# Two layers of a hybrid trunk on one core: the opening's modulation chunks in another order, one chunk between the layers in other memory, and GpSimd's loads behind the chunks

## The reference, cut to what matters

```python
for layer in range(DEPTH):                       # DEPTH = 2
    sh1, sc1, g1, sh2, sc2, g2 = modulation(c or c_ctx, w_mod[layer], b_mod[layer])
    h = rms_norm(x, norm1[layer]) * (1 + sc1) + sh1
    o = even_mixer(h) if layer % 2 == 0 else odd_mixer(h)   # projections, attention, gating
    x = x + g1 * o
    h = rms_norm(x, norm2[layer]) * (1 + sc2) + sh2
    x = x + g2 * ec_moe(h)                       # 16 experts, each picks 64 + 16 rows
y = rms_norm(x, final_norm)
def modulation(cvec, w_mod, b_mod):
    return split(silu(cvec) @ w_mod + b_mod, 6)  # w_mod is 1024 x 6144 for each layer
```

## Time and profile before

| what | us |
|---|---|
| median of 3 runs | 1421.32 |
| lowest and highest of them | 1417.71, 1426.94 |
| the profiled execution, device time | 1414.43 |
| its span, first to last instruction | 1412.3 |
| TensorE busy in it (91%) | 1282.4 |
| VectorE busy (62%) | 877.2 |
| ScalarE busy (52%) | 735.4 |

### The profile page before, as it was taken

One profiled execution on the slowest core, in us unless ns is written; L12 is line 12 of the kernel. 1 busy time (PEld: TensorE's weight loads), 2 busy tenths in 40 slices (PEclk: granted clock), 3 DMA queues, 4 the chain that ended last, 5 costly groups with the idle time before them and its releaser, 6 DMA issues.

```text
span 1412.3 us, 18208 instructions
## 1 busy us (share of the span) xinstructions
PE 1282.4 (91%) x7552; PEld 925.0 (65%) x7552; DVE 877.2 (62%) x1010; ACT 735.4 (52%) x866; POOL 212.1 (15%) x125
## 2 busy tenths in 40 slices
PE   5899988898589999999789999899986999999996
PEld 3796766796356666666459994567954566666662
DVE  3713456524668888888374352454256699999995
ACT  3522037613557777777253214554146677777763
POOL 3000000020102222211020000000202033332220
PEclk9998799999889999999899999799998999999998
DMA  9721073004599999999794222001145999999984
GB/s 359 219 81 32 30 247 129 1 31 178 202 361 380 380 377 375 381 387 397 263 277 120 80 76 87 1 1 62 59 179 210 367 399 383 383 383 384 381 338 165
DMA packets 99606, 322.86 MB, mean 229 GB/s; under 512 B 6367, under 2 KB 30142, under 8 KB 83142
## 3 DMA queue, kind: packets, MB, share of 16 engines
q1 hardware_dynamic: 87360, 283.54, 53.4%
q0 software_dynamic: 8400, 27.58, 7.6%
q10 hardware_dynamic: 3766, 10.58, 1.9%
HBM read 298.20 MB, written 23.49 MB: 228 GB/s over the span
## 4 chain that ended last, share of the span: by engine, by line
PE 67%; DMA 14%; ACT 9%; DVE 8%; issue 2%; SPq 1%; ACTq 0%; DVEq 0%; POOLq 0%
PE psum L889 64%; DMA stage<-in_w_mod 4%; ACT arena L1719 3%; DVE w_lo L1905 3%; DVE arena L2183 2%; DMA xT<-in_moe_w_up 2%; DMA arena<-in_moe_w_up 2%; DMA stage<-in_moe_w_up 2%; ACT w_hi L1788 1%; DMA h_hi<-h_dram,arena 1%; DMA stage<-in_moe_w_gate 1%; DMA arena<-in_moe_w_gate 1%; PE psum L1372 1%; ACT arena L1485 1%; DVE h_lo L1905 1%
## 5 line engine op out<-in xcount | busy, mean ns | idle before, releaser
L889 PE MATMUL psum<-w_hi,h_hi 128*80 128x512 f32 (+1 forms) x848 | 330.2, 389 | 14.4 <-DVE h_lo L1905 10.2
L1905 DVE TENSOR_TENSOR w_lo<-stage,w_hi 128x2048 fp32r<-128x2048 f32 (+1 forms) x120 | 270.9, 2270 | 93.6 <-ACT w_hi L1498 55.9
L889 PE MATMUL psum<-w_lo,h_hi 128*80 128x512 f32 (+1 forms) x848 | 326.0, 384 | 0.0
L889 PE MATMUL psum<-w_hi,h_lo 128*80 128x512 f32 (+1 forms) x848 | 325.7, 384 | 0.0
L889 PE MATMUL psum<-h_hi,w_hi 128*128 128x320 f32 x672 | 211.9, 315 | 5.1 <-DVE h_lo L1955 5.1
L1788 ACT ACTIVATE w_hi<-stage 128x2048 fp32r<-128x2048 f32 x98 | 186.7, 1915 | 45.2 <-PE psum L889 28.7
L889 PE MATMUL psum<-h_lo,w_hi 128*128 128x320 f32 x672 | 210.1, 313 | 0.0
L889 PE MATMUL psum<-h_hi,w_lo 128*128 128x320 f32 x672 | 210.0, 312 | 0.0
L1905 DVE TENSOR_TENSOR w_lo<-arena,w_hi 128x2048 fp32r<-128x2048 f32 x75 | 171.5, 2290 | 33.5 <-ACT w_hi L1788 32.6
L889 PEld LDWEIGHTS psum<-w_hi,h_hi 128*80 128x80 f32 (+1 forms) x848 | 129.8, 153 | 88.8 <-issue 15.3
L854 POOL DMA_INDIRECT acc_dram<-arena x31 | 109.7, 3538 | 429.6 <-ACT arena L1825 230.3
(11 more groups left out here) (253 smaller groups left out, 1329.1 us busy)
## 6 DMA issues: line engine op xcount, KB each, us to landing
stage<-in_w_mod SPq DMA_DIRECT2D x48, 1024.0 KB, 7.6
stage<-in_moe_w_up SPq DMA_DIRECT2D x35, 1024.0 KB, 15.8
stage<-in_moe_w_down SPq DMA_DIRECT2D x32, 1024.0 KB, 16.4
stage<-in_moe_w_gate SPq DMA_DIRECT2D x31, 1024.0 KB, 16.0
arena<-in_moe_w_gate SPq DMA_DIRECT2D x28, 1024.0 KB, 17.4
arena<-in_moe_w_up SPq DMA_DIRECT2D x24, 1024.0 KB, 16.2
arena<-in_moe_w_down SPq DMA_DIRECT2D x21, 1024.0 KB, 14.9
xT<-in_moe_w_down SPq DMA_DIRECT2D x11, 1024.0 KB, 21.1
```

What stands on the lines that cost most here:

```text
L889: return pe.matmul(o, w, x, start=first, stop=last, skip_group_check=True)
L1905: return nc.vector.tensor_tensor(dst, src, hi.bitcast(F32), ALU.subtract)
```

## The change

The lines of the listing here are cut from the diff; the helper functions `mod_before` and `mod_place` are new.

```diff
-SUM_PLACES, OUT_PLACES, X_PLACES = (4,), (5, 6), (7, 8)
-PLACES = 9
+SUM_PLACES, OUT_PLACES, X_PLACES, FRONT_PLACE = (4,), (5, 6), (7, 8), 9
+PLACES = 10
...
-MOD_AT = {"start": [0, 1, 2, 3], "qk": [4, 5], "first scores": [6, 7], (0, "sum"): [8], (0, "root"): [9, 10],
+MOD_AT = {"start": [2, 3, 0, 1], "qk": [4, 5], "first scores": [6, 7], (0, "sum"): [8], (0, "root"): [9, 10],
...
+def mod_before(c):      # the chunk whose turning frees mrow
+def mod_place(c):       # a chunk's number in TensorE's order, for mod_used
...
-    mod("start")
+    for c in MOD_AT["start"][:2]:
+        chunk(c)
     for L in range(LAYERS):
...
         if L > 0:
-            mod("acc")
+            chunk(MOD_AT["acc"][0]), chunk(MOD_AT["acc"][1])
+            chunk(MOD_AT["acc"][2], (FRONT_PLACE, SUM_PLACES[0]))
             chunk(MOD_AT["next norm"][0])
...
+            if (kind, m) == ("q", 0):
+                for c in MOD_AT["start"][2:]:
+                    chunk(c)
...
+            if n == FRONT_PLACE:
+                return arena[:, 0:PIECE]
...
-            filled(pool, ("mod rows", 2))
+            filled(pool, ("mod rows", MOD_AT["start"][-1]))
...
                     emptied(pool, (0, "moe", KD - 1))
+                    pc = piece[("mod", MOD_AT["next norm"][1], 1)]
+                    pool.wait_ge(stage_in[pc["place"]], arrived(pc["p"]))
...
# TensorE
-            for c in MOD_AT["start"]:
-                mod_rows(c)
-                if c:
-                    turn_mod(c - 1)
-                if c == 1:
-                    norm_sum_of_two((0, "norm", 0))
+            mod_rows(scale[0])
+            mod_rows(scale[1])
+            turn_mod(scale[0])
+            turn_mod(scale[1])
+            norm_sum_of_two((0, "norm", 0))
+            mod_rows(shift[0])
+            turn_mod(shift[0])
+            mod_rows(shift[1])
             turn_mod(MOD_AT["start"][-1])
...
# ScalarE
+                    if (L, which) == (0, 0) and k in (4, 6):
+                        modulation("start", slice(k // 2 - 2, k // 2 - 1))
...
+                        if L == 0 and k == 1:
+                            modulation("start", slice(3, None))
...
             squares_for_pool(0, 0, None)
-            modulation("start", slice(0, 2))
+            split(in_keys(0)[0])
             root_of(0, 0)
             modulation("start", slice(2, 3))
-            split(in_keys(0)[0])
-            modulation("start", slice(3, None))
...
# VectorE
-                if name == (1, "norm", 0):
-                    split(in_keys(1)[0])
+                if name[1:] == ("norm", 0):
+                    split(in_keys(name[0])[0])
...
+                        if L == 0 and k == 4:
+                            modulation("start", slice(3, None))
...
-            modulation("start", slice(0, 1))
+            modulation("start", slice(0, 2))
             root_of((0, "norm", 0))
-            modulation("start", slice(1, 3))
-            split(in_keys(0)[0])
-            modulation("start", slice(3, None))
+            modulation("start", slice(2, 3))
```

More of the change, by code:

```diff
@@ L102, in turned_banks @@
     return (512, 512) if STEPS[i] is None else (512, 512, 256)
-MOD_AT = {"start": [0, 1, 2, 3], "qk": [4, 5], "first scores": [6, 7], (0, "sum"): [8], (0, "root"): [9, 10],
+MOD_AT = {"start": [2, 3, 0, 1], "qk": [4, 5], "first scores": [6, 7], (0, "sum"): [8], (0, "root"): [9, 10],
           (0, "rank"): [11], (0, "top"): [12], "acc": [13, 14, 15], "next norm": [16, 17], "cq": [18, 19], (1, "sum"): [20],
           (1, "root"): [21, 22], (1, "rank"): [23], (1, "top"): []}
+def mod_before(c):
+    start = MOD_AT["start"]
+    if c in start:
+        return start[start.index(c) - 1] if start.index(c) else None
+    return c - 1 if c - 1 not in start else start[-1]
+def mod_place(c):
+    start = MOD_AT["start"]
+    return start.index(c) + 1 if c in start else c + 1
 IN = {0: [("q", 1024), ("q", 1280), ("kv", 1536), ("va", 512), ("va", 768), ("u", 0), ("u", 256)],
@@ L173, in plan_psum @@
         one(("x", k), "dve")
-    for c in MOD_AT["start"]:
-        one(("mod rows", c), "act")
-        if c == 2:
-            one(("mod turned", 1), "dve")
-        elif c:
-            one(("mod turned", c - 1), "dve")
-        if c == 1:
-            one((0, "norm", 0), "dve", 2)
+    scale, shift = MOD_AT["start"][:2], MOD_AT["start"][2:]
+    one(("mod rows", scale[0]), "act"), one(("mod rows", scale[1]), "act")
+    one(("mod turned", scale[0]), "dve"), one(("mod turned", scale[1]), "dve")
+    one((0, "norm", 0), "dve", 2)
+    one(("mod rows", shift[0]), "act"), one(("mod turned", shift[0]), "dve"), one(("mod rows", shift[1]), "act")
     one(("mod turned", MOD_AT["start"][-1]), "dve")
@@ L321, in plan_weights, with chunk @@
     after = {"va": lambda m: ("va", m, 2), "kv": lambda m: "v", "ckv": lambda m: "kr", "cq": lambda m: ("cq", 1)}
+    def chunk(c, places=(None, None)):
+        Lc, j = divmod(c, MODS)
+        for half in range(2):
+            piece(("mod", c, half), rows(a["w_mod"][Lc])[:, 4 * half:4 * half + 4, MODC * j:MODC * (j + 1)], False,
+                  ("mod_used", mod_place(c)) if half == 0 else ("mod rows", c), places[half])
     def mod(at):
         for c in MOD_AT[at]:
-            L, j = divmod(c, MODS)
-            for half in range(2):
-                piece(("mod", c, half), rows(a["w_mod"][L])[:, 4 * half:4 * half + 4, MODC * j:MODC * (j + 1)], False,
-                      ("mod_used", c + 1) if half == 0 else ("mod rows", c))
-    mod("start")
-    for L in range(LAYERS):
-        def chunk(c):
-            Lc, j = divmod(c, MODS)
-            for half in range(2):
-                piece(("mod", c, half), rows(a["w_mod"][Lc])[:, 4 * half:4 * half + 4, MODC * j:MODC * (j + 1)], False,
-                      ("mod_used", c + 1) if half == 0 else ("mod rows", c))
+            chunk(c)
+    for c in MOD_AT["start"][:2]:
+        chunk(c)
+    for L in range(LAYERS):
         if L > 0:
-            mod("acc")
+            chunk(MOD_AT["acc"][0]), chunk(MOD_AT["acc"][1])
+            chunk(MOD_AT["acc"][2], (FRONT_PLACE, SUM_PLACES[0]))
             chunk(MOD_AT["next norm"][0])
@@ L1546, in modulation @@
                 for c in MOD_AT[at][part]:
-                    if c > 0:
-                        filled(act, ("mod turned", c - 1))
+                    if mod_before(c) is not None:
+                        filled(act, ("mod turned", mod_before(c)))
                     evacuate(("mod rows", c), mrow[:, :], bank(("mod rows", c)))
```

## The result

The changed kernel takes 1405.18 us (median; 1402.0 to 1409.7) where the kernel before takes 1420.44 in runs beside it (1417.71 to 1426.94): a ratio of 0.9882, 95% interval 0.9853 to 0.9912. (The quotient of the two medians is 0.9893, inside that interval.) That is faster by 1.2% by the ratio and by 1.1% by the medians. One run of the changed kernel took 2506.01 us and one of a repeat of the kernel before 4331.27; ranges, ratios and intervals leave them out, the two medians (1405.18, and 1422.12 of that repeat) include them and would be 1404.70 and 1420.78 without. The forecast was 1412.8, about half that gain, and I had given 0.87 to a change within 1% and 0.10 to a gain of more.

The account below looks back on a forecast made before the run. TensorE, busy 91% of the span, was taken as the bound, with its idle or low-clock time deciding; 2.3 us (opening) plus 6.2 (between the layers) made 8.5, so 1421.3 becomes 1412.8. Range 1404 to 1421, the forecast's own 1409 to 1417.

Parts of the forecast that it names:

- Opening, step 1: Opening: norm sum starts at 26.5, 0.4 us earlier, and VectorE's first step comes at 31.1 instead of 31.51.
- rival B: Clock stays up in both waits: opening 4.2 us, between the layers 8.5, sum 12.7, giving 1408.6; chance 0.11.
- Step 2: Opening: VectorE's scaling starts at 37.2, 3.4 us earlier. Between layers: sum's load 1.6 earlier, addition 0.6 faster, 2.2 together.
- Step 3: Opening: chunk 1 is late next; projection starts 41.6, 2.3 us earlier. Between layers: norm sum ends 2.6 earlier, at 712.9.
- Step 4: Opening: TensorE is slower than the tiles afterwards, so the first projection's start decides; 2.3 us taken.
- Step 5: Opening: GpSimd's loads some 3 us later cost nothing. Between layers: VectorE's first tile ends 721.6, projection starts 6.2 earlier.
- Steps 4 and 7: Between layers: chunks issued 2.2 us earlier, wait for chunk 17 goes; GpSimd's loads start at 717, costing nothing.
- Step 6: Between layers: projection ends 737.8 instead of 743.95; next weight's split, 2.6 us earlier at 737.9, just fits.
- rival C: A later load or low spell of the clock takes up the gain before the end: about 1421; chance 0.08.
- A: Between layers: clock takes the norm sum's gain, projection starts 3.6 us earlier instead of 6.2; 1415.4; chance 0.17.
- D: Clock stays at 1.2 GHz through all 96 matmuls of both first projections: 11.2 us slower, 1432.5; chance 0.06.
- E: Chunk 15's second piece lands late or ScalarE's copies hold up GpSimd: 6 to 7 us left, 1414.5; 0.58 with the forecast.

Follow-up runs that it names:

- `opening_only`: Changed kernel with the two edits between the layers taken out, only the opening's new order left: 1413.70 us, ratio 0.9938.
- `no_front`: Changed kernel with chunk 15 back in the staging slots, GpSimd's loads still behind chunk 17: 1408.38 us, ratio 0.9900.
- the two filled ones: Changed kernel with idle transposes in four waits, 1409.63 us, and with them in the two opening waits only, 1407.22 us.
- `after_again`: Changed kernel once more, unchanged, for a second trace: 1406.13 us, ratio 0.9888.
- `no_gate`: Changed kernel with GpSimd's loads between the layers no longer held back behind chunk 17: 1410.76 us, ratio 0.9924.
- `before_filled`: Kernel before with 18 idle transposes in TensorE's wait ahead of the opening's first turning of a chunk: 1422.08 us, ratio 1.0002.
- `between_only`: Kernel before with only the part between the layers (chunk 15's new place, GpSimd's loads behind chunk 17): 1410.79 us, ratio 0.9931.
- `after_third`: Changed kernel once more, unchanged, for a third trace: 1405.4 us, ratio 0.988.
- `after_filled`: Changed kernel with idle transposes in four waits of TensorE, in the opening and between the layers: 1409.63 us, ratio 0.9916.

## Why the prediction was right in its mechanisms and short in its size

**Opening, step 1** is the step that failed. It took the norm sum's 4.47 us over from the earlier trace rows. The norm sum took 2.40, in two of three traces of the changed kernel and in all four of `opening_only`, `no_front` and the two filled ones; 3.91 in `after_again` and 4.07 in `no_gate`. In the five unfilled traces of the old order it is 4.08 to 4.47. TensorE's idle time ahead of it is shorter in the new order (1.06 us in the first trace of the changed kernel, 3.13 ahead of the turning of the chunk before), and in `before_filled` filling that idle time went with 2.40. Shorter idle time alone is no guarantee: 1.46 us stood ahead of 4.07 and of 2.40. What else decides is open. My rival B had this ("opening 4.2", which is exactly what the first pair shows: 43.87 against 39.69), but I gave it 0.11 and tied it to a second event between the layers that did not happen.

The first projection's start gives the opening's error in two parts. With the low norm sum the new order starts it at 41.91 and 41.73, where I had 41.6; with the fast one at 39.19 to 40.03, 39.7 by the mean of six traces. So the norm sum's clock is worth some 2 us of the error. The rest, 1.3 us, is my starting point: the old order starts it at 43.87 in the trace that I had, and at 45.2 by the mean of its four traces and `between_only`.

**Step 2** follows: VectorE's first step came at 29.04 instead of 31.1, and the scaling at 34.98 instead of 37.2, 2.2 earlier than forecast for a 2.1 earlier start. **Step 3** was right in kind: the copy of chunk 1 behind two tiles of ScalarE, then the turning, then the projection. Its last piece landed at 37.03, later than my 35.5, and in this trace that is the end of the gain: a still faster norm sum would have brought nothing. (In `after_third` ScalarE's copy stood behind the two tiles without waiting for TensorE, so there the tiles still decided.) **Step 4**: from first matmul to the end of the projection 16.5 us before (43.87 to 60.36) and 16.5 after (39.69 to 56.20), so the start decided. **Step 5**: GpSimd's loads started at 38.47 and nobody waited.

**Between the layers** the sum of 6.2 was near: 6.5 by the table in the first pair, 6.1 by the means. In the first pair 0.8 of the 6.5 lies ahead of the last addition (23.4 against 22.6 us from matmul 3600 to its issue), where the change has nothing to act on. Counted from that issue, the projection started 5.5 us earlier in the first pair (727.88 - 685.04 against 720.03 - 682.66) and 6.6 by the means of four and three traces.

*Step 2.* The addition in HBM was worth more than my 0.6. From its issue to ScalarE's next issue it takes 6.8 to 7.1 us in the seven traces with chunk 15 in the stage slots, and 5.1 to 5.7 in the seven with its new place: 1.1 to 2.0 less, above my 0.6 and up to my upper bound of 2. The queues are not quiet in either. What changed is which part of the addition the bulk loads run beside. In the seven traces of the new place SyncE's packets go on for the first 2.2 to 3.8 us and then stop, and the addition's own packets begin at 2.0. In the seven others SyncE's packets begin 1.9 us behind the issue and outlast the addition, whose own begin at 3.7 to 4.1. By the DMA view (packets, MB, share of 16 engines), q0 being the addition and q1 SyncE's loads, before from 688.9 to 691.9, then the changed kernel from 682.66 to 684.6 and from 686.6 to 688.4:

```profile
q0 software_dynamic: 96, 0.33, 54.8%
q1 hardware_dynamic: 279, 0.57, 51.2%
```

```profile
q1 hardware_dynamic: 260, 0.51, 67.2%
```

```profile
q0 software_dynamic: 36, 0.08, 24.1%
```

The Trainium skill, "DMA: Bandwidth & Descriptors", section "Anatomy of one DMA", puts most of a transfer's fixed time on the receipt. It says nothing there of loads beside the transfer, so my sentence that by it the addition would gain nothing did not follow from it, and it did not hold here.

*Step 3*, counted from the issue of the last addition: the norm sum ended 30.5 us behind it before (706.73 + 8.82 - 685.04) and 28.0 after (701.81 + 8.82 - 682.66), so 2.5 earlier; forecast 2.6. The clock came back in the middle of the turnings, as assumed: 3.62 and 2.08, beside 3.45 and 1.91 in the earlier trace rows. *Steps 4 and 7*: no wait for chunk 17, and no one waits for GpSimd's loads. But the issue of chunk 16 came 16.3 us behind that of the last addition where it had been 17.5, so 1.2 earlier and not 2.2.

*Step 5* came out only in part, and that is the load of `("cq", 0)`: it is issued behind chunk 16, landed at 710.02 while the norm sum ended at 710.63, ScalarE's split waits for it, and VectorE sat idle 0.50 us for ScalarE before its half (711.99 to 714.28), with the root's next step behind that. It takes most of the difference between 5.5 and my 6.2. *Step 6* holds to 0.2 us: the projection with its turning of a chunk is through at 736.3, and the next weight's split, which starts at 733.79 and takes 2.36, at 736.15.

**The sum.** In stretches of the table, means of four and three traces: 5.4 in the opening, 6.1 between the layers, 0.8 in the last, less 2.4 lost again in 250 to 3600 and 0.2 at the start: 9.8 in all, which is the mean difference of the profiled executions too (1416.7 against 1406.9). My 8.5 is 1.3 short of that: 3.1 too little for the opening, 0.1 too much between the layers, 0.8 from the last stretch, and 2.4 lost behind the opening, which would be rival C in part. In that stretch the traces of the two kernels overlap (596.5 to 598.2 against 596.7 to 601.3), and so they do in the last, so neither is shown to belong to the change. That 8.5 is so near to 9.8 is therefore partly luck.

**The reference** was the second error, and the larger one. The medians differ by 15.3 us and the profiled executions by 9.8; the 5.5 between are in no trace. I took the median's 6.9 us above the profiled execution as a fixed offset. Over the runs of one group the time goes with the mean granted clock that each run lists: eighteen runs of before have a correlation of -0.92, from 1414.14 us at 0.950 to 1426.34 at 0.944, and a straight line through them gives 6.3 us for 0.005 of clock. All four profiled executions of before lie at 0.949 or 0.950, above the mean of 0.947 of those eighteen; the three of the changed kernel lie at 0.956, 0.955 and 0.952, and its five runs in that group at 0.953 to 0.957, mean 0.955. For that 0.008 of clock the line gives about 10 of the 15 us; a line through runs shows that the two go together, not which causes which. Before's four lie 2.4 to 6.9 us under medians of 1420.4 and 1421.3, the changed kernel's three from 0.5 under to 4.6 over 1405.2 and its like. T3 holds, with one limit: even before's four traces are faster than most of its runs, and what the slower runs do differently, no trace here shows. That the clock is lower in them is measured; in which stretch it is low, and why the new order has less of it also in runs without a trace, stays open. Filling one wait of the old order left the median and the mean clock of its runs where they were (0.948, beside 0.947), so nothing shows that wait alone to be the reason.

A slip in the prediction's chances belongs here too: it explains the 0.10 for a gain of over 1% by half of rival B, which at 0.11 is 0.055.

The other rivals: A did not happen (the norm sum ended 2.5 earlier), D did not (20 matmuls at 0.50 behind the first wait, against the 96 it needed), E did not (chunk 15 had landed when TensorE came to it, if narrowly).

## What to carry to other kernels

When a change moves work on TensorE from behind a wait to behind other work, forecast it at both clock levels that the trace shows and ask which idle time has gone; take the next bound (here chunk 1's landing, 37.03) from the queue, since it ends what the faster clock can give. A sum against one profiled execution should be held to other profiled executions: read the granted clock of each run before adding the distance to the median as a constant. And when a transfer in HBM is on the critical path, look at which bulk loads run beside it and when: loading chunk 15 earlier, so that its packets ended well before the addition did, took one wait away and made the addition itself shorter.

## What was unexpected of the hardware

- The addition in HBM of one expert's output takes 5.1 to 5.7 us where SyncE's 1 MB loads end 2.2 to 3.8 us behind its issue, and 6.8 to 7.1 where they begin 1.9 us behind it and outlast it (seven traces each).
- In the six traces of the old order `("q", 0)` has landed at 35.66, 37.78, 37.34, 37.04, 37.16 and 37.74. The third issue of a chunk's load, in the first 9 us, takes 3.69, 5.04, 4.49, 4.51, 3.67 and 3.66 us in them and does not decide it.
- Eighteen idle transposes (2.19 us) ahead of the norm sum went with 2.40 us for it instead of 4.08 to 4.47 (one trace), and the kernel's median stays the same; in `after_filled` TensorE got a full clock over 24.90 to 49.90 and 0.65 over the last 30.9 us. Whether the one causes the other is not shown: the last stretch takes 21.9 to 26.9 us in the unfilled kernels too.
